# Mixture of experts in a two-block network: which side an expert runs on, and in what pieces its weights are loaded

## The reference, cut to what matters

```python
scores = softmax(x @ router_w)                 # 512 tokens, 16 experts
sel = scores + router_b
_, gidx = top_k(group_score(sel), 1)           # the best of 4 groups of 4 experts
_, eidx = top_k(where(in_group, sel, -inf), 2) # two experts of that group
w = take(scores, eidx); w = w / sum(w)
for e in range(16):
    h = silu(x @ w1[e]) * (x @ w3[e])          # 1024 -> 512
    out = out + gates[:, e:e + 1] * (h @ w2[e])  # 512 -> 1024
```

## Time and profile before

| | |
|---|---|
| median of 3 runs | 2528.93 us (2523.74 to 2532.64) |
| the profiled execution's own time | 2532.06 us |
| its span | 2530.2 us |
| PE busy | 2362.1 us, 93% |
| first product of the first job | 593.34 us from the span's start |
| first product of the last job | 903.89 us |
| PE idle in L1343, waiting for expert weights | 49.0 us in 5 waits |

### The profile page before, as it was taken

The page is one execution under the profiler, slowest core; times in us unless marked ns, Lnnn a source line. Parts: engine busy times, 40 slices in busy tenths (PEclk is TensorE's granted clock), DMA queues, the critical chain, the costliest instruction groups (busy, mean ns, idle before and its releaser), DMA issues.

```text
span 2530.2 us, 28944 instructions
## 1 busy us (share of the span) xinstructions
PE 2362.1 (93%) x10176; PEld 1662.1 (66%) x10177; DVE 968.8 (38%) x1756; ACT 522.6 (21%) x1097; POOL 134.0 (5%) x150
## 2 busy tenths in 40 slices
PE   6999999985689889899999999899999989999999
PEld 2564455642234338668888888576675778888888
DVE  7331256552000023662434433333333354335521
ACT  2200045531111133452111100112212202111100
POOL 1000046200001110000000000000000000000000
PEclk9999999887889999989999999899999999999999
DMA  9301122257977891102222222131121212232220
GB/s 339 126 9 50 33 78 114 77 225 261 382 273 300 289 354 59 42 26 74 77 83 83 84 84 100 67 100 58 41 91 51 65 67 83 92 91 84 84 102 31
DMA packets 81185, 299.24 MB, mean 118 GB/s; under 512 B 9024, under 2 KB 9024, under 8 KB 80464
## 3 DMA queue, kind: packets, MB, share of 16 engines
q1 hardware_dynamic: 75312, 272.14, 31.0%
q0 software_dynamic: 5792, 26.00, 2.7%
HBM read 283.94 MB, written 14.16 MB: 118 GB/s over the span
## 4 chain that ended last, share of the span: by engine, by line
PE 85%; DVE 6%; ACT 3%; issue 3%; SPq 2%; DMA 1%; DVEq 0%; POOL 0%; POOLq 0%; ACTq 0%
PE products L1513 39%; PE products L944 7%; PE products L1123 6%; PE products L1343 6%; PE products L1418 3%; PE products L1361 3%; PE products L1660 2%; PE products L1174 2%; PE products L1595 2%; PE products L1030 1%; PE products L1077 1%; PE products L1252 1%; PE products L1468 1%; PE products L1142 1%; PE products L1087 1%
## 5 line engine op out<-in xcount | busy, mean ns | idle before, releaser
L1513 PE MATMUL products<-normed,weights_and_work 128*128 128x264 f32 (+1 forms) x1520 | 347.7, 384 | 0.0
L1513 PEld LDWEIGHTS products<-normed,weights_and_work 128*128 128x128 f32 x1520 | 288.7, 190 | 49.0 <-issue 3.4
L1756 ACT ACTIVATE weights_and_work<-products 128x256 f32<-128x256 f32 (+4 forms) x243 | 109.4, 466 | 605.9 <-PE products L1513 156.4
L1343 PE MATMUL products<-weights_and_work 128*64 128x512 f32 x768 | 178.3, 625 | 49.7 <-DMA weights_and_work<-in_experts 49.0
L1513 PE MATMUL products<-weights_and_work,mixed 128*128 128x256 f32 (+1 forms) x800 | 182.3, 382 | 0.8 <-ACT weights_and_work L1756 0.8
L1343 PEld LDWEIGHTS products<-weights_and_work 128*64 128x64 f32 x768 | 64.8, 145 | 161.5 <-issue 160.5
L1513 PEld LDWEIGHTS products<-weights_and_work,mixed 128*128 128x128 f32 x800 | 151.9, 190 | 24.3 <-ACT weights_and_work L1756 1.6
L1123 PE MATMUL products<-weights_and_work,normed 128*128 128x512 f32 x352 | 154.8, 601 | 8.4 <-DVE normed L2166 8.4
L1513 PE MATMUL products<-weights_and_work 128*128 128x256 f32 (+1 forms) x672 | 151.0, 385 | 8.2 <-DVE residual L3051 5.2
L1513 PE MATMUL products<-weights_and_work,normed 128*128 128x264 f32 (+1 forms) x704 | 155.6, 383 | 0.0
L1513 PE MATMUL products<-normed,mixed 128*128 128x264 f32 (+1 forms) x672 | 154.2, 383 | 0.0
(11 more groups left out here) (518 smaller groups left out, 2923.6 us busy)
## 6 DMA issues: line engine op xcount, KB each, us to landing
weights_and_work<-in_weights SPq DMA_DIRECT2D x303, 512.0 KB, 4.3
weights_and_work<-in_experts SPq DMA_DIRECT2D x192, 512.0 KB, 5.4
results<-weights_and_work SPq DMA_DIRECT2D x8, 512.0 KB, 5.5
residual<-in_x POOLq DMA_DIRECT2D x1, 2048.0 KB, 15.9
weights_and_work<-in_dft_half POOLq DMA_DIRECT2D x1, 2048.0 KB, 8.5
token_rows<-mixed SPq DMA_DIRECT2D x4, 512.0 KB, 3.1
normed<-results SPq DMA_DIRECT2D x4, 512.0 KB, 6.7
mixed<-results SPq DMA_DIRECT2D x4, 512.0 KB, 7.6
```

The lines of the kernel that those rows point to most:

```text
L1343: m = pe.matmul(ps[UNIT * b:UNIT * (b + 1), side, :], job_t[:, k, UNIT * b:UNIT * (b + 1)], expert_w[b][:, s, at:at + 512], start=(k == 0) ...
L1513: m = pe.matmul(bank(p, n), left(k), right(k), start=(fresh and k == 0), stop=(k == kt - 1), skip_group_check=True)
L1756: act.activation(out, src, ACT.Copy, scale=scale).then_inc(bank_free[p.bank], 1)
```

## The change

1. **Sides.** DVE sorts the experts by units, long ones first (expert 0 is forced to the front and expert 1 to the end), and cuts the row in the middle. The first part goes to side 0 in that order, the rest to side 1 in the opposite order, short ones first. On the inputs above, side 0 runs experts 0, 10, 6, 7, 9 from jobs 0, 1, 5, 7, 9 (11 units), and side 1 runs 1, 15, 14, 13, 12, 8, 5, 4, 3, 2, 11 from jobs 0, 1, 2, 3, 4, 5, 6, 7, 8, 9, 10 (12 units).
2. **Loads in parts.** An expert is loaded in three parts of four tiles, one for each phase. Experts that start at the same job are interleaved by phase: phase 0 of both, phase 1 of both, phase 2 of both. Of the 48 parts, 6 (experts 0 and 1) are written out, and 42 are turns of the SP loop. The four semaphores `e_landed` now belong to the tile's place in its part.
3. **Tables.** DVE computes a table of 48 loads in columns. PE turns it into rows with 9 small matmuls, and DVE copies it to one partition as integers.
4. **Earlier work.** The zeros are set during the attention and written out amid the second modulation's weight tiles. Experts 0 and 1 are both loaded before the token rows are stored. POOL gathers the first job's rows before it reads the number of jobs. PE reads three numbers per job in place of one. The squares of the router's norm move to another place (`sq_2`).

```diff
 # SP
+                if n == mod2 + RING + 9:
+                    sp.wait_ge(zero_set, 1)
+                    for i in range(2 * ST):
+                        sp.dma_start(results[i * P:(i + 1) * P, :], zeros).then_inc(results_zeroed, 16)
...
+            by_phase = d["experts"].rearrange("e (g i) p t -> (e g) i p t", g=PHASES)
+            def first_of(n):
+                phase, e = n // 2, n % 2
+                for i in range(PHASE_TILES):
+                    s = slots[PHASE_TILES * phase + i]
+                    if n:
+                        sp.wait_ge(e_landed[i], 16 * n)
...
+                    sp.dma_start(expert_w[e][:, s, :], by_phase[PHASES * e + phase, i]).then_inc(e_landed[i], 16)
+            first_of(0)
+            ready(sp, r["OT", ST - 1][1])
+            for n in range(1, 2 * PHASES):
+                first_of(n)
...
-            with sp.Fori(2, EXPERTS) as it:
-                e = sp.value_load(order_i[0:1, bass.ds(it, 1)], min_val=0, max_val=EXPERTS - 1)
-                landed_by = sp.value_load(landed_i[0:1, bass.ds(it, 1)], min_val=0, max_val=16 * EXPERTS)
-                to = sp.value_load(buffer_i[0:1, bass.ds(it, 1)], min_val=0, max_val=RING * TILE)
-                for i, s in enumerate(slots):
-                    passed_by = sp.value_load(after_i[0:1, i, bass.ds(it, 1)], min_val=1, max_val=MAX_JOBS * EXPERT_TILES)
+            with sp.Fori(2 * PHASES, LOADS) as it:
+                part = sp.value_load(loads_i[0:1, 0, bass.ds(it, 1)], min_val=0, max_val=LOADS - 1)
+                to = sp.value_load(loads_i[0:1, 1, bass.ds(it, 1)], min_val=0, max_val=(2 * RING - PHASE_TILES) * TILE)
+                landed_by = sp.value_load(landed_i[0:1, bass.ds(it, 1)], min_val=0, max_val=16 * LOADS)
+                for i in range(PHASE_TILES):
+                    passed_by = sp.value_load(loads_i[0:1, 2 + i, bass.ds(it, 1)], min_val=1, max_val=MAX_JOBS * EXPERT_TILES)
                     sp.wait_ge(e_passed, passed_by)
-                    sp.wait_ge(e_landed[s], landed_by)
-                    sp.dma_start(weights_and_work[:, bass.ds(to + s * TILE, TILE)], d["experts"][e, i]).then_inc(e_landed[s], 16)
+                    sp.wait_ge(e_landed[i], landed_by)
+                    sp.dma_start(weights_and_work[:, bass.ds(to + i * TILE, TILE)], by_phase[part, i]).then_inc(e_landed[i], 16)
 # POOL
-            pool.wait_ge(jobs_ready, 1)
-            n_jobs = pool.value_load(n_jobs_i[0:1, 0:1], min_val=MIN_JOBS, max_val=MAX_JOBS)
...
             gather(slice(0, 1), 1)
+            pool.wait_ge(jobs_ready, 1)
+            n_jobs = pool.value_load(n_jobs_i[0:1, 0:1], min_val=MIN_JOBS, max_val=MAX_JOBS)
 # PE
+                for n, (p, columns, count) in enumerate(((r["landings"], landing_col, PHASES), (r["loads"], load_col, 6))):
+                    fill(p)
+                    pe.wait_ge(columns_set, n + 1)
+                    for v in range(count):
+                        m = pe.matmul(ps[0:1, p.bank, 64 * v:64 * (v + 1)], columns[:, v:v + 1], ident[:, 0:64], start=True, stop=True)
+                    finish(p, m)
...
-                    landing = pe.value_load(landing_i[0:1, bass.ds(it, 1)], min_val=16, max_val=16 * EXPERTS)
+                    landing = [pe.value_load(landing_i[0:1, phase, bass.ds(it, 1)], min_val=16, max_val=16 * LOADS)
+                               for phase in range(PHASES)]
 # DVE, router()
+                link(tt_(key, units, size_bias, ALU.add))
+                link(tt_(sooner_t, bcast(key, 1, EXPERTS), bcast(key, 2, EXPERTS), ALU.is_gt))
+                link(tt_(sooner_t, sooner_t, bcast(units, 1, EXPERTS), ALU.mult))
+                link(dve.tensor_reduce(begun_before, sooner_t, AX_X, ALU.add))
+                link(stt(past, begun_before, 2.0, units, ALU.mult, ALU.add))
+                link(ts(past, past, total, None, ALU.subtract))
+                ts(side, past, 0.0, None, ALU.is_ge)
+                link(ts(past, past, 0.0, None, ALU.max))
+                link(tt_(begun_before, begun_before, past, ALU.subtract))
...
```

More of the change, by code:

```diff
@@ L60 @@
 EXPERT_TILES = 12
+PHASES, PHASE_TILES = 3, 4
+LOADS = 16 * PHASES
 UNIT = 64
@@ L2387, in attentions @@
                 maxima(0, "A")
+                dve.memset(zeros, 0.0).then_inc(zero_set, 1)
                 dve.wait_ge(lam_exp, 1)
@@ L2564, in router @@
-                link(tt_(over, over, bcast(landing_e, 1, JOBS), ALU.mult))
-                link(dve.tensor_reduce(landing_f, over, AX_X, ALU.max))
-                link(ts(last_f, end[:, EXPERTS - 1:EXPERTS], -UNIT / 2.0, end[:, HALF - 1:HALF], ALU.add, ALU.max))
+                link(ts(first, begun_before, 1.0 / UNIT, None, ALU.mult))
+                link(tt_(sooner_t, bcast(first, 1, EXPERTS), bcast(first, 2, EXPERTS), ALU.is_lt))
+                link(dve.tensor_reduce(sooner, sooner_t, AX_X, ALU.add))
@@ new lines, in router @@
+                link(tt_(same_t, bcast(first, 1, EXPERTS), bcast(first, 2, EXPERTS), ALU.is_equal))
+                link(dve.tensor_reduce(same, same_t, AX_X, ALU.add))
+                link(stt(within, same, -1.0, side, ALU.add, ALU.mult))
+                link(stt(load_base, sooner, float(PHASES), within, ALU.mult, ALU.add))
+                for phase in range(PHASES):
+                    ins = stt(load_no[:, phase], same, float(phase), load_base, ALU.mult, ALU.add)
+                link(ins)
@@ new lines, in router @@
+                ts(landing_e, load_no, 16.0, 16.0, ALU.mult, ALU.add)
+                link(ts(begun_e, first, partition, None, ALU.is_le))
+                link(tt_(load_t, landing_e, bcast(begun_e, 1, PHASES), ALU.mult))
+                dve.tensor_reduce(landing_col, load_t, AX_X, ALU.max).then_inc(columns_set, 1)
+                dve.wait_ge(columns_set, 1)
+                for phase in range(PHASES):
+                    ts(load_ids[:, phase], lane[:, 0:EXPERTS], float(PHASES), float(phase), ALU.mult, ALU.add)
+                    ts(after_e[:, phase], first, float(EXPERT_TILES), float(PHASE_TILES * phase + 1 - EXPERT_TILES), ALU.mult, ALU.add)
+                    ts(buffer_e[:, phase], side, float(RING * TILE),
+                       float((START["ab_qk"] + PHASE_TILES * phase) % RING * TILE), ALU.mult, ALU.add)
@@ L2567, in router @@
+                dve.wait_ge(columns_set, 2)
+                p = r["landings"]
+                ready(dve, p)
+                link(tt_(end, begun_before, units, ALU.add))
+                link(dve.tensor_reduce(last_f, end, AX_X, ALU.max))
                 link(ts(count[:, 0:1], last_f, 1.0 / UNIT, None, ALU.mult))
                 link(ts(last_f, count[:, 0:1], 1.0, None, ALU.subtract))
-                dve.tensor_copy(landing_i, landing_f)
+                dve.tensor_copy(landing_i[0:1].rearrange("p g j -> p (g j)"), ps[0:1, p.bank, 0:64 * PHASES]).then_inc(bank_free[p.bank], 1)
```

119 lines of the change are left out of this document (49 added, 70 removed).

## The result

The changed kernel takes 2549.61 us (median of 4 runs, 2547.03 to 2550.69), the kernel before in the same series 2530.02 us. The ratio is 1.0074, with a 95% interval of 1.0056 to 1.0091: slower by 0.74%. Between the medians lie 19.6 us. The profiled execution took 2549.75 us, its span is 2547.9 us.

What follows compares the result with a forecast made beforehand. PE, busy 93% of the span, was taken as the bound, idling for expert weights at SP's issuing pace. Parts +15.5 us, all other terms 0, on 2532.06 gave 2547.6 for the profiled execution, 2544 us median; range 2532 to 2558.

Steps and rivals of the forecast that it cites:

- PE waits for SP, SP for nothing: Expert loop: SP no longer waits for tiles passed; PE waits about 65 us for expert weights at jobs 1, 5, 7, 9.
- some 11 for slow clock: Jobs: of 77 us beyond 12 undisturbed jobs, some 11 are PE's slow clock, leaving about 65 of waits.
- Parts, +15.5 us: SP's expert loading: at 7.5 us per part, the last job ends at 942.3 instead of 926.8, 15.5 us later.
- The argument that an expert's three parts take 22.0 us, less than a job: SP's loop: a job with one new expert needs 22.0 us of issuing against 22.67 us of PE.
- The break-even price of 7.08 us per part: SP's loop: a part must cost less than 7.08 us for a gain; 7.34 was expected from the rows.
- Zeros, 0 with ends 0 and +10: Eight zero writes ahead of modulation tiles in SP's queue: taken as 0, at worst 10 us if DVE's tile were late.
- Tables, 0: DVE's table work before the first job: PE turns the first rows near 590.4 as before; 0, ends -1.5 and +3.
- Sides, no job saved: Sorting experts onto sides: 12 jobs before and after, with four double changes (both sides change expert) instead of five.
- Three reads per job on PE, 0: PE's job loop: two more reads take 1.3 us, exposed only at jobs 10 and 11; 0, ends 0 and 2.6.
- The rival of the full gain: Expert loop: interleaved parts remove all five waits, gaining 58.5 us, median 2470 us; chance 0.03.

Runs made afterwards that it cites:

- whole_sorted: The changed kernel with loads of whole experts (one part of 12 tiles) instead of three parts of four: 2507.18 us, ratio 0.9907 to the kernel before.
- few_reads: The changed kernel with 4 table reads by SP per part instead of 7: 2513.67 us, ratio 0.9922 to the kernel before.
- more_reads: The changed kernel with one more, unused table read by SP per part: 2571.55 us, ratio 1.0160 to the kernel before.
- both pairs: Changed kernel (2549.61 us) against itself with zeros written late (2556.18); kernel before (2530.02) against itself with only the zeros early (2524.74).
- six_few_old_sides: six_few with the kernel before's sides (even experts on side 0, odd on side 1, in order of number): 2503.59 us, ratio 0.9898 to the kernel before.
- six_few: The changed kernel with two parts of six tiles per expert and 4 table reads per part: 2488.16 us, ratio 0.9816 to the kernel before.
- six_tiles: The changed kernel with two parts of six tiles per expert instead of three of four: 2517.21 us, ratio 0.9935 to the kernel before.

## Why the prediction was right, point by point

The prediction said 2544 us, 2532 to 2558, slower. 2549.61 lies inside, but two of its terms were off in opposite directions. With the jobs as measured and the zeros at nothing, the median would have been near 2528.93 + 27.2 = 2556 us. That it came within 6 us of the forecast is in part luck; the sign and the mechanism of the parts are not.

- **PE waits for SP, SP for nothing: right.** The wait for tiles passed went from 48.6 to 1.8 us. PE's waits stand at jobs 1, 5, 7 and 9 in up to four pieces and come to 62.6 us (65 predicted). At jobs 2 and 4 there are 0.5 us each, where none was foreseen. What was undersized is what comes beyond the waits, "some 11 for slow clock": measured 360.6 - 12 x 22.67 - 62.6 = 25.9 us. Since SP's pace sets the end, slower products take their time out of the waits.
- **Parts, +15.5 us: right mechanism, mis-sized; it measured +27.2.** The jobs were put at 349.0 us (942.3 - 593.3) and took 360.6. (Against whole_sorted, which has the same sides, the parts cost 40.0 us of jobs.) Of the 11.6 us, 37 x (7.69 - 7.5) = 7.1 are the price of a part. It consists of a base of 7.50 us instead of 7.34, because the third and fourth tile of a turn take 1.30 and 1.36 us rather than 1.26, and of slow reads, 0.6 to 1.3 us in about one turn of four. Another 1.4 us come before the second turn (598.00 - 584.39 = 13.6 us instead of 605.5 - 593.3 = 12.2), and 3.0 behind the 39th turn's first issue (944.96 - 882.70 = 62.3 us instead of 59.3). The argument that an expert's three parts take 22.0 us, less than a job, fails by the same price: they took 23.1. The break-even price of 7.08 us per part is bracketed: few_reads at 6.8 us is faster than the kernel before, the change at 7.69 and more_reads at 8.24 are slower.
- **Zeros, 0 with ends 0 and +10: wrong.** This is the step that failed: "DVE takes such a tile at 432.35 without a wait before it, and POOL does the others, off the chain". POOL's work is off the chain, but its time decides what DVE's work beside it costs. The zeros were worth 6.4 us in the profiles of both pairs; another 2.9 of the 8.95 us by which the first product came sooner stood there before the zeros. The term's ends, 0 and +10, had excluded a gain.
- **Tables, 0: right.** From the start of the attention's output projection, at 513.25 before and 503.82 after, to the first job it took 80.1 us before and 80.6 after.
- **Sides, no job saved: right**; the tail's 8.9 us and the 15 us of six_few_old_sides show what the sorting gives. That it pays once loading is quick was not seen.
- **Three reads per job on PE, 0: right.** Jobs 10 and 11 follow without a gap: 899.45 to 922.09 is 22.64 us.
- **The rival of the full gain** (parts remove the waits; 2470 us) was rightly put behind the price of a part. Its mechanism is real: six_few, whose parts are cheap, came to 2488 us and keeps 3.8 to 4.4 us of each wait. What the rival missed is that the transfers take over then.

## What to carry to other kernels

A load in smaller pieces pays the head of the loop once per piece: here 2.3 us on top of 1.26 per tile. First work out the issuing engine's time per piece, then divide it by the time in which the consumer uses the piece. With 23.1 against 22.67 us no backlog was worked off, and 42 us were lost against whole experts. With 4 table reads and pieces of six tiles, sorted sides, early zeros and interleaving together gained 1.8% on the kernel before, and 19 us on whole experts with as few reads. Before splitting a load, replace numbers that can be counted up by a constant: five reads fewer per piece of six tiles were worth 29 us.

Once the issue is cheap, the transfers are the next bound, and then it matters how many double changes there are and how close together they stand.

## What the runs showed of the hardware

- A table read by SP costs 0.57 to 0.66 us of its queue (0.57 by more_reads, 0.66 from one read's start to the next in the earlier trace rows), and one turn in four to six takes 0.6 to 1.3 us longer (10 of 41 turns in the change, 7 of 41 in more_reads).
- Transfers of 512 KB tiles, with a gather and a scatter between them, ran at 346 GB/s with at most four allowed on their way, 405 with six and 411 with twelve, in the window 718 to 795. The parts differ in size too between the first and the second, so the step from 346 to 405 is not shown to come from the number alone.
- DVE's norm of the heads (TENSOR_TENSOR, 256 elements), where it begins while POOL's addition over 1024 elements runs, ends 0.28 us after POOL's. This holds for all 28 such meetings in the 13 profiles. It took 2.10 us where it began late in POOL's addition (six_tiles, 384.54, POOL's from 384.01 to 386.35) and 2.51 at most, against 0.42 to 0.43 without. So it looks like a wait for POOL's end, not like slower work. What the two share there was not tried apart.
- Which of the two happens is decided by when POOL's tiles land. At 428 it costs 6.4 us, the granted clock at half for 10.2 us behind PE's wait of 1.94 us included.
